# The input projection of a hybrid encoder layer by Strassen's seven products, on one core

## Chip, core and metric

One core of one Trainium2 chip runs the whole program. The metric is the device time of one execution in microseconds (us). The engines are named as the profile names them: PE (TensorE), DVE (VectorE), ACT (ScalarE), POOL (GpSimd), and SP (SyncE, which here only issues DMAs).

## What is computed

The reference is one encoder layer for 1024 tokens of width 2048, all in float32. Cut to what matters here:

```python
h = rmsnorm(x, norm_mix_g)                              # x: 1024 x 2048
proj = jnp.einsum('bsd,dn->bsn', h, w_in)               # w_in: 2048 x 6160
na_q, na_k, na_v, ml_q, ml_k, ml_v, ml_o, gates = jnp.split(proj, IN_SPLITS, axis=-1)
na_out = rmsnorm(neighbourhood_attention(na_q, na_k, na_v, rpb), na_norm_g)
ml_out = mlstm_mixer(ml_q, ml_k, ml_v, ml_o, gates, b_gates, conv_w, conv_b, ml_norm_g)
x = x + concatenate([na_out, ml_out]) @ w_out
x = x + expert_choice_ffn(rmsnorm(x, norm_ffn_g), w_router, w_gate, w_up, w_down)
return rmsnorm(x, final_norm_g)
```

The widths of the eight parts are 1024, 1024, 1024, 512, 512, 1024, 1024 and 16. The first seven make 6144 columns, 12 blocks of 512. Only this first projection, what it writes and the start of the attention behind it are changed.

## The kernel before

**Precision.** A float32 product is made of three products of a faster type (fp32r): each operand is split into a high part, a copy rounded to fp32r on ACT, and a low part, the difference of the value and the high part, on DVE. The product is high x high + high x low + low x high.

**The projection.** The activations a_hi and a_lo (16 pieces of 128 inputs by 1024 tokens) are made once at the start from xT, with the gain g_mix, and stay in SBUF. The scale 1/rms of each token (rstd) is applied when a result leaves PSUM. The weights stream through a ring of four tiles of 1024 columns (two pieces of 128 inputs x 512 columns): SP loads raw, ACT makes whi (`high`, L902), DVE makes wlo (`low`, L1226). There are 12 blocks of 512 columns in two kinds. Six are made in rows (`rows_block`, L1718 to L1720): activations are the stationary operand, weights move, the result has tokens on partitions, and ACT evicts it (L910). Six are made in features (`feats_block`, L1740): weights are stationary, activations move, the result has features on partitions, and DVE evicts it (L1329, L1333). Each block is 16 pieces x 8 PSUM banks x 3 = 384 matmuls with 512 moving columns. Between the two kinds stand the 96 gate matmuls (L1761). POOL's queue stores the evicted tiles to the DRAM tensors scr_rows and scr_feats (L656).

**Beside it.** In the first feature blocks DVE computes the gates' scans (L1258 to L1314) and in the last four the convolution of ml_q and ml_k: for each of 8 blocks of 128 features, one tensor_scalar (L1355) and four scalar_tensor_tensor (L1358) of 1024 elements, and a Silu on ACT.

**Behind it.** The neighbourhood attention reads q, k, v and the bias back from DRAM. SP waits for the last projection result before it issues the first of these loads:

```python
sp.wait_ge(S["bank_ready"], 8 * BLK)
for m in stsem:
    sp.wait_ge(m, 32 * (BLK - 2))
fetch_skew(0)
fetch_qk(0)
fetch_v(0)
```

The order of the work on each engine is the order in which the program text of that engine's function is written; semaphores join them. Nothing is reordered by a planner.

Of the kernel before, what the change touches and what calls it, by code (L numbers as in the profile page):

```python
# [16 lines left out]
P = 128  # L17
# [13 lines left out]
BW = 512  # L31
BLK = 12
ROWBLK = 6
# [20 lines left out]
MLU = 16 * MLH  # L54
ROOM = 19456
# [33 lines left out]
def trunk(nc, t):  # L89
    ctx = ExitStack()  # L90
    with ctx:
# [20 lines left out]
        proj = ExitStack()  # L112
        raw = sb("raw", [P, RING, 1024], F32, proj)
        whi = sb("whi", [P, RING, 1024], F32R, proj)
        wlo = sb("wlo", [P, RING, 1024], F32R, proj)
        stage = sb("stage", [P, 4, BW], F32, proj)
        t0 = sb("t0", [P, 1024], F32, proj)
        t1 = sb("t1", [P, 1024], F32, proj)
        t2 = sb("t2", [P, 1152], F32, proj)
        rstd_bc = sb("rstd_bc", [P, 1024], F32, proj)  # L120
        t3 = stage[:, 0:2, :].rearrange("p a b -> p (a b)")
        wide = ExitStack()
        a_hi = sb("a_hi", [P, KD, SEQ], F32R, wide)
        a_lo = sb("a_lo", [P, KD, SEQ], F32R, wide)
        gmix = sb("gmix", [P, KD], F32, wide)
        ssum = sb("ssum", [P, KD], F32, wide)
        wg_raw = sb("wg_raw", [P, GWC], F32, wide)
        wg_hi = sb("wg_hi", [P, GWC], F32R, wide)
        wg_lo = sb("wg_lo", [P, GWC], F32R, wide)
        wide.close()  # L130

        gate = ExitStack()
        gate.enter_context(nc.sbuf_tensor("under_wide", [P, 2 * KD * SEQ + 2 * KD + 3 * GWC], F32))
        g_bias = sb("g_bias", [P, 2], F32, gate)
        b_last = sb("b_last", [64, TT], F32, gate)
        c_last = sb("c_last", [64, TT], F32, gate)
        m_next = sb("m_next", [64, TT + 2], F32, gate)
        m_prev = sb("m_prev", [64, TT], F32, gate)
        m_end = sb("m_end", [64, TT], F32, gate)
        decay = sb("decay", [64, TT], F32, gate)  # L140
        cw = sb("cw", [P, 2, CONVW + 1], F32, gate)
        gate.close()


        proj.close()
# [96 lines left out]
        for n in ("const_in ident_done raw0 raw1 raw2 raw3 xt0 xt1 xnat0 xnat1 xn_sq hT_hi hT_lo w_hi w_lo w_used "  # L242
                  "bank_ready bank_staged st0 st1 st2 st3 stage_free meansq_done rstd_done rstd_out rstd_bc_in "
                  "wg_hi wg_done gates_ready gates_copied gpad_zero gb_in grows_out dve_step "
                  "act_step pool_step mask_done acc_free conv_in conv_free silu_done conv_out "
                  "pool_past dve_past pad_in rep_out cols_ready cols_out nq0 nq1 nkv0 nkv1 nb0 nb1 colm_in nmask_done "
# [13 lines left out]
        xhalf = [t2[:, 0:1024], rstd_bc[:, :]]  # L260
# [120 lines left out]
        def chunk_free(eng, b, m):  # L381

            if m >= 4:
                eng.wait_ge(S["w_used"], 7 * b + (m - 3))
            elif m < 3:
                eng.wait_ge(S["w_used"], 7 * b + (m - 2))
            else:
                eng.wait_ge(S["bank_ready"], 8 * b)
# [6 lines left out]
        def o_consumed(eng, q):  # L395

            i, k = q // KD, q % KD
            if k == KD - 1:
                eng.wait_ge(S["bank_ready"], 8 * BLK + 4 * i + 4)
            else:  # L400
                eng.wait_ge(S["w_used"], 7 * BLK + (KD - 1) * i + k + 1)
# [5 lines left out]
        def _(sp):  # L407
            def fetch(b, m):

                if not (isinstance(b, int) and b == 0 and m < 4):  # L410
                    sp.wait_ge(S["w_lo"], CPB * b + (m - 3))
                src = t["w_stream"][bass.ds(CPB * b + m, 1), :, :].rearrange("a p c -> (a p) c")
                sp.dma_start(raw[:, m % RING, :], src).then_inc(rawsem[m % RING], 16)

            sp.dma_start(gmix[:, :], t["g_mix"]).then_inc(S["const_in"], 16)
            sp.dma_start(wg_raw[:, 0:KD * 16], t["w_gates"]).then_inc(S["const_in"], 16)

            for m in range(CPB):
                fetch(0, m)
                for k in (2 * m, 2 * m + 1):  # L420
                    if k >= 2:
                        sp.wait_ge(S["hT_lo"], k - 1)
                    sp.dma_start((t0, t1)[k % 2][:, :], t["xT"][k * P:(k + 1) * P, :]).then_inc(xtsem[k % 2], 16)
            with sp.Fori(1, BLK) as b:
                for m in range(CPB):
# [1686 lines left out]
```

## Time and profile before

| what | value |
|---|---|
| median of 3 runs | 2973.68 us (2972.35 to 2974.95) |
| profiled execution: time | 2972.88 us |
| profiled execution: span | 2971.3 us |
| granted PE clock, mean | 0.973 |
| PE busy | 2781.7 us (94%) |
| DVE busy | 1583.1 us (53%) |
| ACT busy | 1324.5 us (45%) |
| POOL busy | 374.5 us (13%) |
| DMA, mean | 222 GB/s |

The profiled execution lasts 1.6 us longer than its span, which begins with the first instruction and ends with the last. A busy share is an average over stages with different limits, so the reader should look at the share of each engine in the stretch that is changed, here the first 1083 us.

### The profile page before, as it was taken

What the parts mean: (1) busy time and instruction counts of PE and PEld (TensorE: products, weight loads), DVE (VectorE), ACT (ScalarE), POOL (GpSimd) and SP (SyncE); (2) the same over time, 40 slices, a digit from 0 to 9 for tenths busy, and PEclk for the clock granted to TensorE, in tenths of its full rate; (3) what the DMA queues carried; (4) which work ended last, traced back from release to release, by engine and by line L of the source; (5) the groups of instructions that cost most, each with busy time, mean ns of one, the idle gap of its engine ahead of it and who ended that gap; (6) DMA issues with size and microseconds to landing.
All of it is one profiled execution on the core that took longest, in us unless ns stands there. A gap on an engine that the chain in (4) does not pass through costs nothing.

```text
span 2971.3 us, 33520 instructions
## 1 busy us (share of the span) xinstructions
PE 2781.7 (94%) x12738; PEld 2281.5 (77%) x12738; DVE 1583.1 (53%) x1679; ACT 1324.5 (45%) x1458; POOL 374.5 (13%) x593
## 2 busy tenths in 40 slices
PE   8999999999999989989999944999999999999992
PEld 7888888888888867768777733888888888888881
DVE  4110111311233326674332358888888888888883
ACT  5111111201111115654232323777777777777773
POOL 1200000020011023571010101010000000000000
PEclk9999999999999999999999977999999999999996
DMA  8322212122222238534354455999999999999987
GB/s 308 93 76 78 76 51 78 57 98 78 78 104 101 78 117 245 179 103 139 131 167 135 162 177 197 381 396 405 401 388 406 401 405 404 403 403 403 402 319 269
DMA packets 193516, 660.53 MB, mean 222 GB/s; under 512 B 24025, under 2 KB 49128, under 8 KB 170608
## 3 DMA queue, kind: packets, MB, share of 16 engines
q1 hardware_dynamic: 169088, 564.52, 50.2%
q0 software_dynamic: 24304, 94.39, 9.7%
q8 instruction: 74, 1.21, 0.2%
q14 instruction: 50, 0.41, 0.0%
HBM read 585.99 MB, written 72.79 MB: 222 GB/s over the span
## 4 chain that ended last, share of the span: by engine, by line
PE 87%; issue 4%; DVE 3%; POOL 3%; DMA 1%; SPq 1%; ACT 0%; POOLq 0%; DVEq 0%; ACTq 0%
PE ps L2024 23%; PE ps L1740 17%; PE ps L1718 6%; PE ps L1720 6%; PE ps L1719 6%; PE ps L1961 4%; PE ps L1963 4%; PE ps L1962 4%; PE ps L2047 4%; PE ps L2045 4%; PE ps L2046 4%; PE ps L2003 1%; PE ps L1942 1%; PE ps L1782 1%; PE ps L1761 1%
## 5 line engine op out<-in xcount | busy, mean ns | idle before, releaser
L1635 DVE TENSOR_TENSOR elo<-eraw,ehi 128x2048 fp32r<-128x2048 f32 x384 | 874.4, 2292 | 137.1 <-ACT ehi L1146 130.6
L1146 ACT ACTIVATE ehi<-eraw 128x2048 fp32r<-128x2048 f32 x384 | 733.2, 1919 | 246.8 <-PE ps L2024 163.8
L1226 DVE TENSOR_TENSOR wlo<-raw,whi 128x1024 fp32r<-128x1024 f32 x96 | 117.6, 1225 | 704.9 <-ACT whi L902 704.8
L902 ACT ACTIVATE whi<-raw 128x1024 fp32r<-128x1024 f32 x96 | 101.7, 1059 | 732.6 <-PE ps L1740 393.5
L2024 PE MATMUL ps<-ehi,xh 128*128 128x512 f32 x960 | 373.5, 389 | 0.0
L2024 PE MATMUL ps<-elo,xh 128*128 128x512 f32 x960 | 373.4, 389 | 0.0
L1718 PE MATMUL ps<-whi,a_hi 128*128 128x512 f32 x768 | 299.9, 390 | 11.3 <-DVE a_lo L1236 11.3
L1719 PE MATMUL ps<-wlo,a_hi 128*128 128x512 f32 x768 | 299.6, 390 | 0.0
L1720 PE MATMUL ps<-whi,a_lo 128*128 128x512 f32 x768 | 299.5, 390 | 0.0
L2024 PE MATMUL ps<-ehi,xl 128*128 128x512 f32 x960 | 256.6, 389 | 0.0
L1740 PE MATMUL ps<-a_hi,whi 128*128 128x512 f32 x768 | 236.8, 389 | 1.8 <-DVE t L1258 1.6
L1740 PE MATMUL ps<-a_lo,whi 128*128 128x512 f32 x768 | 236.5, 389 | 0.0
L1740 PE MATMUL ps<-a_hi,wlo 128*128 128x512 f32 x768 | 236.4, 389 | 0.0
L1509 DVE TENSOR_TENSOR olo<-oraw,ohi 128x512 fp32r<-128x512 f32 x128 | 88.5, 697 | 249.9 <-ACT ohi L1073 249.8
L2024 PEld LDWEIGHTS ps<-ehi,xl 128*128 128x128 f32 x960 | 180.2, 188 | 37.4
L2024 PEld LDWEIGHTS ps<-elo,xh 128*128 128x128 f32 x960 | 180.2, 188 | 37.4
L2024 PEld LDWEIGHTS ps<-ehi,xh 128*128 128x128 f32 x960 | 180.2, 188 | 37.4
L1961 PE MATMUL ps<-ohi,a_hi 128*128 128x512 f32 x512 | 204.9, 400 | 3.6 <-DVE mh L1469 3.6
L2045 PE MATMUL ps<-ehi,hh 128*128 128x512 f32 x512 | 202.9, 396 | 0.0
L1963 PE MATMUL ps<-ohi,a_lo 128*128 128x512 f32 x512 | 200.7, 392 | 0.0
L1962 PE MATMUL ps<-olo,a_hi 128*128 128x512 f32 x512 | 200.5, 392 | 0.0
L2047 PE MATMUL ps<-ehi,hl 128*128 128x512 f32 x512 | 199.5, 390 | 0.0
(246 smaller groups left out, 3892.3 us busy)
## 6 DMA issues: line engine op xcount, KB each, us to landing
eraw<-in_w_gate SPq DMA_DIRECT2D x256, 512.0 KB
eraw<-in_w_up SPq DMA_DIRECT2D x256, 512.0 KB
eraw<-in_w_down SPq DMA_DIRECT2D x128, 1024.0 KB
raw<-in_w_stream SPq DMA_DIRECT2D x96, 512.0 KB
oraw<-in_w_stream SPq DMA_DIRECT2D x128, 256.0 KB
scr_rows<-stage POOLq DMA_DIRECT2D x48, 256.0 KB, 2.3
scr_feats<-stage POOLq DMA_DIRECT2D x48, 256.0 KB, 2.3
t<-in_xT SPq DMA_DIRECT2D x16, 512.0 KB, 5.6
```

Of the source, the lines that this page charges most:

```text
L1146: act.activation(ehi[:, p % ERING, :], flat2(eraw[:, 2 * (p % EDEEP):2 * (p % EDEEP) + 2, :]), ACT.Copy)\
L1635: dve.tensor_tensor(elo[:, p % ERING, :], flat2(eraw[:, 2 * (p % EDEEP):2 * (p % EDEEP) + 2, :]), ehi[:, p % ERING, :].bitcast(F32), ALU.s ...
L1718: pe.matmul(ps[:, n, :], xs, hi, start=(k == 0), stop=False)
L1719: pe.matmul(ps[:, n, :], xs, lo, start=False, stop=False)
L1720: last = pe.matmul(ps[:, n, :], src_lo[:, k, n * P:(n + 1) * P], hi, start=False, stop=(k == KD - 1))
L1740: last = pe.matmul(ps[:, n, :], w, src[:, k, h * BW:(h + 1) * BW], start=(k == 0 and w is hi and src is a_hi), stop=(k == KD - 1 and w is lo))
L1961: pe.matmul(bank, xs, hi, start=(k == 0), stop=False)
L1962: pe.matmul(bank, xs, lo, start=False, stop=False)
L1963: last = pe.matmul(bank, a_lo[:, KORD[k], n * P:(n + 1) * P], hi, start=False, stop=(k == KD - 1))
L2024: last = pe.matmul(gu_bank(e, c), a[:, k, :], w[:, p % ERING, c * BW:(c + 1) * BW], start=(k == 0 and a is hi and w is ehi), stop=(k == KD ...
L2045: pe.matmul(y_bank(e, c), hh[:, h, :], ehi[:, p % ERING, at], start=(k == 0), stop=False)
L2047: last = pe.matmul(y_bank(e, c), hl[:, h, :], ehi[:, p % ERING, at], start=False, stop=(k == KE - 1))
```

## The change

**Strassen.** The projection is cut into 12 runs (`RUNS`). A run is one half of the tokens (512) and one pair of column blocks (1024 columns). With the input dimension cut into halves as well, it is a product of two 2 x 2 block matrices, made by seven products of half size instead of eight. A product i has 8 chunks k (128 inputs x 512 columns) and two token tiles: 8 x 2 x 3 = 48 matmuls. `B11` and `B22` are quarters of the weights that stay for a run; products 1, 2, 5 and 6 stream a chunk through a ring of four slots (wst) and add b11 or b22 to it; product 3 adds b22 to b11 in place; products 0 and 4 use b11 and b22 as they are (SUMMED is 1, 2, 3, 5, 6; g is the run, i the product, k the chunk):

```diff
+def sum_on_dve(g, i, k):
+    return i in SUMMED and k % 4 == 3 and g not in (0, 5, 6)
...
+        def weight_sum(eng, g, i, k):
...
+            a = weights_of(g, i, k)
+            other = b11[:, k, :] if i in (1, 2) else b22[:, k, :]
+            return eng.tensor_tensor(a, a, other, ALU.subtract if i in (2, 6) else ALU.add)
```

POOL makes 390 of these 480 sums, DVE 90. The sum is split into whi (ACT) and wlo (DVE) as before, now in tiles of 512 columns and a ring of four such tiles:

```diff
-    act.activation(whi[:, m % RING, :], raw[:, m % RING, :], ACT.Copy).then_inc(S["w_hi"], 1)
+    if q >= RING:
+        consumed(act, q - RING)
+    act.activation(whi[:, q % RING, :], weights_of(g, i, k), ACT.Copy).then_inc(S["w_hi"], 1)
...
-    dve.tensor_tensor(wlo[:, m % RING, :], raw[:, m % RING, :], whi[:, m % RING, :].bitcast(F32), ALU.subtract)
+    dve.tensor_tensor(wlo[:, q % RING, :], weights_of(g, i, k), whi[:, q % RING, :].bitcast(F32), ALU.subtract)
```

The activations' seven combinations for a token half are made in runs 0 (first half), 5 and 6 (second half): POOL multiplies xT by the gain (`gain`, 16 operations for a half), DVE and POOL add (`act_sum`, 8 and 12), ACT and DVE split (28 each). They lie in seven regions of SBUF (acts).

**Results.** A product ends in one of four pairs of PSUM banks. ACT copies three of the seven to SBUF (`keep_product`), DVE adds the others to them (`combine`, 16 operations of 128x512 in a run, one operand in PSUM), ACT multiplies by rstd (`stage_c`, 8 in a run). All runs are in rows. In the six feature runs PE turns each result by 32 transposes against the identity, ACT evicts them, and SP stores them:

```diff
+            def turn_c(g, c):
+                if is_rows(g):
+                    return
+                for t_ in range(2):
...
+                    for f in range(4):
...
+                        last = pe.transpose(bank, stage[:, 2 * (c % 2) + t_, f * P:(f + 1) * P], ident[:, :])
```

The matmuls of a chunk, and the gates, which are now 16 plain float32 matmuls for each half instead of 96 of fp32r:

```diff
-            with pe.Fori(1, ROWBLK) as b:
-                rows_block(b, a_hi, a_lo)
-            with pe.Fori(ROWBLK, BLK) as b:
-                feats_block(b)
+                for t_ in range(2):
+                    pe.matmul(bank, xh_, hi, start=(k == 0), stop=False)
+                    pe.matmul(bank, xh_, lo, start=False, stop=False)
+                    last = pe.matmul(bank, xl_, hi, start=False, stop=(k == 7))
...
+            for k in range(KD):
+                last = pe.matmul(gate_bank(6 * half_), wg[:, at:at + P], flat3(actr[region(half_, 6 - k // 8)][:, k % 8, :, :]),
+                                 start=(k == 0), stop=(k == KD - 1))
```

**Beside it.** The gates' scans stand in run 7, between its chunks 16 and 38. The convolution stands in runs 8 to 11, two feature blocks in each: one of its five operations behind each of the chunks 6 to 10, and 34 to 38:

```diff
+                if g >= CONVRUN:
+                    c, n = divmod(8 * i + k, 28)
+                    if 6 <= n < 11:
+                        conv(2 * (g - CONVRUN) + c, n - 6)
```

**Behind it.** The first loads of the attention wait for product 4 of the last run, no longer for the last product; the last three stores of results are issued behind them:

```diff
-            sp.wait_ge(S["bank_ready"], 8 * BLK)
+            sp.wait_ge(S["bank_ready"], 2 * (7 * (NRUN - 1) + 5))
             fetch_skew(0)
...
             fetch_v(1)
+            store_c(NRUN - 1, 1)
+            store_c(NRUN - 1, 2)
+            store_c(NRUN - 1, 3)
```

**The order on the engines.** DVE in a feature block with convolution before (wlo is a weight's low part, t is the convolution's accumulator):

```order
L1226 TENSOR_TENSOR wlo<-raw,whi 128x1024 x2
L1355 TENSOR_SCALAR t<-t,cw 128x1024
L1358 SCALAR_TENSOR_TENSOR t<-t,cw 128x1024 x4
L1226 TENSOR_TENSOR wlo<-raw,whi 128x1024 x2
L1355 TENSOR_SCALAR t<-t,cw 128x1024
L1358 SCALAR_TENSOR_TENSOR t<-t,cw 128x1024 x4
L1226 TENSOR_TENSOR wlo<-raw,whi 128x1024
L1333 TENSOR_TENSOR stage<-ps,rstd_bc 128x512 x8
```

And DVE now, from the start of one of the runs 8 to 11 (wst and b are a streamed and a kept chunk of weights, tmp_b and stage hold partial results):

```order
L1610 TENSOR_TENSOR wlo<-b,whi 128x512 x3
L1656 TENSOR_TENSOR tmp_b<-ps,tmp_b 128x512
L1658 TENSOR_TENSOR stage<-ps,stage 128x512
L1656 TENSOR_TENSOR tmp_b<-ps,tmp_b 128x512
L1658 TENSOR_TENSOR stage<-ps,stage 128x512
L1610 TENSOR_TENSOR wlo<-b,whi 128x512 x4
L1771 TENSOR_SCALAR t<-t,cw 128x1024
L1610 TENSOR_TENSOR wlo<-b,whi 128x512
L1774 SCALAR_TENSOR_TENSOR t<-t,cw 128x1024
L1610 TENSOR_TENSOR wlo<-wst,whi 128x512
L1774 SCALAR_TENSOR_TENSOR t<-t,cw 128x1024
L455 TENSOR_TENSOR wst<-wst,b 128x512
```

The five operations of a convolution no longer stand in one piece between tiles that serve 48 matmuls each; they stand between chunks that serve 6 matmuls each, and the additions of results and the weight sums have joined them.

POOL had only DMA issues in the projection; now, in run 0, it has gains (L894), weight sums (L455) and activation sums (L493):

```order
L894 TENSOR_SCALAR actr<-actr,gmix 128x512 x16
L455 TENSOR_TENSOR wst<-wst,b 128x512 x13
L493 TENSOR_TENSOR actr<-actr 128x2x256
L455 TENSOR_TENSOR wst<-wst,b 128x512
L493 TENSOR_TENSOR actr<-actr 128x2x256
L455 TENSOR_TENSOR wst<-wst,b 128x512
```

Every one of these stands ahead of a chunk or of an activation that PE waits for.

## Rows read from the trace of the kernel before

**Rows 1.** The page, part 1 (busy us, share of the span, instructions):

```profile
PE 2781.7 (94%) x12738; PEld 2281.5 (77%) x12738; DVE 1583.1 (53%) x1679; ACT 1324.5 (45%) x1458; POOL 374.5 (13%) x593
```

**Rows 2.** Windows: length; busy us of PE, PEld, DVE, ACT, POOL; clock; DMA:

```profile
240.00:530.00 290.00, 290.00 (x1281) 240.01 (x1280) 33.10 (x27) 48.37 (x54) 12.96 (x24) 1.00 0.20 70
...
530.00:600.00 70.00, 68.41 (x300) 55.96 (x299) 27.59 (x32) 19.95 (x22) 8.88 (x17) 1.00 0.19 71
```

**Rows 3.** PE's timeline and the chain of waits: start, duration, what:

```profile
2.42 6.23 DMA t<-in_xT
...
11.29 0.77 PE L1718 MATMUL ps<-whi,a_hi 128*128 128x512 f32 x1 [11.29 <-DVE a_lo L1236]
...
536.01 22.24 PE ps L1761 x96
...
1739.60 3.62 PE ps L1942 x8
...
1821.42 3.66 PE ps L2003 x16
...
2824.43 43.52 PE ps L2024 x192
```

**Rows 4.** The end of the projection and the start of the attention, timeline:

```profile
1082.23 0.61 PE L1740 MATMUL ps<-a_hi,wlo 128*128 128x512 f32 x2
1095.85 4.18 PE L1782 MATMUL ps<-nak,naq 128*128 128x384 f32 x6 [13.00 <-DMA nak<-scr_feats]
...
1090.25 0.99 POOL L757 TENSOR_TENSOR bias<-skew,nmask 128x384 f32<-128x384 f32 x1
...
1098.42 0.61 ACT L1004 ACTIVATE prob<-prob,ntop 128x384 f32<-128x384 f32 x1 [55.59 <-DVE ntop L1386]
```

**Rows 5.** Groups by line, DVE (busy us, mean ns, idle before and its releaser):

```profile
L1226 DVE TENSOR_TENSOR wlo<-raw,whi 128x1024 fp32r<-128x1024 f32 x96 | 117.6, 1225 | 704.9 <-ACT whi L902 704.8
L1509 DVE TENSOR_TENSOR olo<-oraw,ohi 128x512 fp32r<-128x512 f32 x128 | 88.5, 697 | 249.9 <-ACT ohi L1073 249.8
L1333 DVE TENSOR_TENSOR stage<-ps,rstd_bc 128x512 f32<-128x512 f32 x32 | 21.4, 689 | 59.6 <-PE ps L1740 50.9 <-POOLq L660 8.2
L1358 DVE SCALAR_TENSOR_TENSOR t<-t,cw 128x1024 f32<-128x1024 f32 x32 | 41.1, 1285 | 1.1
```

**Rows 6.** Groups by line, POOL and ACT:

```profile
L757 POOL TENSOR_TENSOR bias<-skew,nmask 128x384 f32<-128x384 f32 x48 | 46.6, 1002 | 59.9 <-DMA skew<-scr_rpb_rep 59.4
L812 POOL TENSOR_TENSOR qs<-qs,mq 128x1024 f32<-128x1024 f32 x2 | 4.7, 2365 | 0.0
L798 POOL TENSOR_SCALAR mh<-mh,rsm 128x256 f32<-128x256 f32 x16 | 8.8, 553 | 0.1
L806 POOL TENSOR_SCALAR na_out<-na_out,nrs 128x1024 f32<-128x1024 f32 x8 | 9.3, 1174 | 0.0
L1073 ACT ACTIVATE ohi<-oraw 128x512 fp32r<-128x512 f32 x128 | 80.7, 631 | 258.6 <-PE ps L1963 258.5
```

**Rows 7.** Timeline, DVE beside POOL, in the mLSTM stage:

```profile
1252.29 0.73 POOL L801 TENSOR_TENSOR mh<-mh,mo 128x256 f32<-128x256 f32 x1
...
1252.65 0.64 DVE L1482 SCALAR_TENSOR_TENSOR mh<-mh,rsm,mo 128x256 f32<-128x256 f32 x1
1252.99 0.55 POOL L769 TENSOR_SCALAR kw<-kn,cols 128x128 f32<-128x128 f32 x1
...
1320.02 1.12 POOL L806 TENSOR_SCALAR na_out<-na_out,nrs 128x1024 f32<-128x1024 f32 x1
1320.07 1.21 DVE L1434 TENSOR_TENSOR qkw<-st,wexp 128x128 f32<-128x128 f32 x1 [0.19 <-POOL wexp L778]
```

**Rows 8.** The instructions of L1434, L769 and L1482: ns min/median/max, and when they start:

```profile
L1434 DVE TENSOR_TENSOR qkw<-st,wexp x64: 282/293/1205, 1218.1 to 1329.5; 128x128 f32<-128x128 f32 x64
...
L769 POOL TENSOR_SCALAR kw<-kn,cols x56: 363/372/547, 1205.2 to 1325.7; 128x128 f32<-128x128 f32 x56
...
L1482 DVE SCALAR_TENSOR_TENSOR mh<-mh,rsm,mo x16: 485/634/968, 1252.7 to 1339.6; 128x256 f32<-128x256 f32 x16
```

More of the change, by code:

```diff
@@ L111, in trunk @@
         sb("even", [P, 64])
[L112 to L145, printed above, removed]
         def place(at, *items):
@@ new lines, in sum_done, with slot, streamed, weights_of @@
+        def sum_done(eng, g, i, k):
+            if sum_on_dve(g, i, k):
+                eng.wait_ge(S["w_sum_v"], SUMS_V[chunk(g, i, k)])
+            else:
+                eng.wait_ge(S["w_sum_p"], SUMS_P[chunk(g, i, k)])
+        def slot(g, i, k):
+            return wst[:, k % RING, :]
+        def streamed(eng, g, i, k):
+            eng.wait_ge(rawsem[k % RING], 16 * ((32 * g + STREAMED[i] + k) // RING + 1))
+        def weights_of(g, i, k):
+            if i in (0, 3):
+                return b11[:, k, :]
+            return b22[:, k, :] if i == 4 else slot(g, i, k)
@@ L407, in _, with w_block, fetch_b11 @@
         def _(sp):
[L408 to L413, printed above, removed]
+            def w_block(b, m):
+                return t["w_stream"][CPB * b + m, :, :]
+            def fetch_b11(g, m):
+                if g:
+                    sp.wait_ge(S["w_lo"], chunk(g - 1, 3, 2 * m + 1) + 1)
+                    sp.wait_ge(wbsem[m], 32 * g)
+                sp.dma_start(flat3(b11[:, 2 * m:2 * m + 2, :]), w_block(2 * RUNS[g][1], m)).then_inc(wbsem[m], 16)
@@ new lines, in gain, with row_scale @@
+            def gain(half_, k):
+                pool.wait_ge(rxsem[k // 2], 64 * half_ + 64)
+                for b in range(2):
+                    a = flat3(actr[region(half_, 6 - b)][:, k, :, :])
+                    pool.tensor_scalar(a, a, gmix[:, 8 * b + k:8 * b + k + 1], 0.0, ALU.mult, ALU.add).then_inc(S["x_gained"], 1)
+            def row_scale(half_):
+                four = slice(4 * half_, 4 * half_ + 4)
+                pool.wait_ge(S["meansq_done"], half_ + 1)
+                pool.tensor_tensor(rstd[:, four], meansq[:, four], half[:, 0:4], ALU.pow).then_inc(S["rstd_done"], 1)
+                pool.wait_ge(S["rstd_done"], half_ + 1)
+                pool.dma_start(t["rstd_d"][half_ * BW:(half_ + 1) * BW].rearrange("(t p) -> p t", p=P), rstd[:, four],
+                               allow_slow_non_contiguous=True).then_inc(S["rstd_bc_in"], 16)
@@ L923, in _ @@
-            for m in range(3):
-                high(1, m)
-            act.wait_ge(S["rstd_done"], 1)
-            evict_rows(0)
-            for first, end, func in ((1, ROWBLK - 2, ACT.Copy), (ROWBLK - 2, ROWBLK, ACT.Sigmoid)):
-                with act.Fori(first, end) as b:
-                    for m in range(3, CPB):
-                        high(b, m)
-                    for m in range(3):
-                        high(b + 1, m)
-                    evict_rows(b, func)
-            high(ROWBLK, 3)
@@ L955, in _ @@
-            for m in range(3):
-                high(ROWBLK + 2, m)
-            def feats_high(b, last):
-                for m in range(3, CPB):
-                    high(b, m)
-                    if m in (5, 7):
-                        q = (m - 5) // 2
-                        act.wait_ge(S["conv_free"], 2 * b + (q - 2 * (ROWBLK + 2) + 2))
-                        act.activation(t0[:, :], t0[:, :], ACT.Silu, bias=cw[:, q, CONVW:CONVW + 1]).then_inc(S["silu_done"], 1)
-                if not last:
-                    for m in range(3):
-                        high(b + 1, m)
@@ L1275, in _, with gates_sum @@
+            def gates_sum(x):
+                r, way = ways[x]
                 dve.tensor_tensor_scan(out=t1[r, ::way], data0=t3[r, :], data1=t1[r, ::way], initial=0.0,
```

1090 lines of the change are left out of this document (727 added, 363 removed).

## The prediction

> **What bounds the kernel now.** I read the page first. PE is busy for 94% of the span, DVE for 53%, POOL for 13% [rows 1]. The average says little, so I went to the windows: from 240 to 530 us PE is busy for all of the 290 us at the full clock, DVE for 33 and POOL for 13 [rows 2]. The groups by line say the same from the other side: DVE sits idle 704.9 us before wlo, waiting for ACT [rows 5], and ACT in turn waits for PE to free the ring. So the projection is a row of matmuls that nothing delays. The timeline puts it from 11.3 to 1082.8 us [rows 3, 4], 1071.5 us. A matmul costs 43.52/192 = 0.2267 us [rows 3]; 4608 of them and the 22.24 us of gates make 1066.9, so 4.6 us are lost in stalls. Behind it PE stands still for 13 us, until nak has landed, and the first softmax runs at 1098.4 [rows 4].
>
> **PE's work.** Strassen takes 12 x 7 x 48 = 4032 matmuls in place of 4608: 576 x 0.2267 = 130.6 us less. The features are turned by 6 x 4 x 8 = 192 transposes of 128x128; 16 such take 3.66 us [rows 3], so they add 43.9. The gates were 22.24; now they are 32 plain float32 matmuls of 512 columns. Four of that kind (each leaves two records) take 3.54 to 3.62 us [rows 3], so 0.89 each and 28.3 in all, 6.1 more. PE's work falls by 130.6 - 43.9 - 6.1 = 80.6 us. If nothing held PE up, that would be the gain, and the 4.6 us of stalls besides.
>
> **What each run asks of DVE and POOL.** A run is 336 matmuls, 76.2 us, 83.5 with its 32 transposes. DVE makes 56 lows and, in the nine runs where it helps, 10 sums, 66 x 0.697 = 46.0 (olo is the same form [rows 5]), and 16 additions of results at 0.689 [rows 5], 11.0: 57.0 us. POOL makes 30 sums there, 40 in runs 0, 5 and 6. For a 128x512 sum I interpolate between 1.002 for 384 and 2.365 for 1024 elements [rows 6]: 1.275 us, 38 or 51 us a run. ACT makes 56 highs at 0.631 [rows 6], 35, and some 14 to 22 copies of like size, 10 to 15: below 52 us, not the bound. Taken one by one, every engine fits under PE.
>
> **They are not independent.** At 1320.07 a DVE operation with two SBUF inputs, whose median is 0.293 us [rows 8], takes 1.21: POOL began a 1.12 us one at 1320.02, and DVE ends 0.14 us after it [rows 7]. The other triple shows both ways: DVE, begun at 1252.65 during POOL's mh, ends 0.27 after POOL, and POOL's kw, begun at 1252.99, ends 0.25 after DVE, in 0.55 in place of 0.37 [rows 7, 8]. So the two exclude each other while they stream, and only the first 0.12 to 0.16 of each is hidden. By that a waiting low takes its streaming time after POOL's end, 0.53 us (512 elements more cost 1.225 - 0.697 [rows 5]), and a waiting sum 1.275 - 0.12 = 1.155 after DVE's: 1.69 us a pair. A chunk of PE's is 6 x 0.2267 = 1.36 us. Additions from PSUM have one SBUF input; such DVE operations are not held, and POOL can work beneath them.
>
> The page SBUF — State Buffer of the Trainium skill (section SBUF: two separate sides) has a rule that speaks against this change: GpSimd and a DVE operation with two SBUF inputs take one port pair in turn, as an exclusive lock "held for the full instruction". The trace agrees that they take turns, but not that the whole time counts: DVE ended 0.14 us after POOL where it takes 0.293 alone [rows 7, 8]. Taken in full, a pair would cost 1.97 us, not 1.69.
>
> **The stalls, run by run.** Each is the time by which DVE with its waits exceeds PE's 76.2 or 83.5. A wait for a sum can cost DVE nothing (it falls into idle time or an addition) up to 1.155. POOL holds the pair for about 45% of a run, so I take 0.65 to 0.8 a sum, 20 to 24 us.
> - Runs 1 and 2 (rows): 57.0 + 22 = 79 us, 3 over each; the ring is only four chunks, 4.1 us ahead. Together **6**.
> - Runs 3 and 4 (features): 79 lies under 83.5, but the summed products come in blocks of three and two: 1.5 each, **3**.
> - Runs 8 and 9: a convolution is 4 x 1.285 [rows 5] and a tensor_scalar near 0.7, two a run, 11.7: 91 against 83.5, **15** for both. Runs 10 and 11 are in rows: 89 against 76.2, **26**. Before, this work was free: DVE had the time of 48 matmuls for each tile.
> - Run 7: from 530 to 600 DVE is busy 27.6 us [rows 2], of which four lows and one gate copy are not the scans; 22 us are. They stand in chunks 16 to 38. 79 + 22 less 3 of lead: 98, **22**.
> - Run 5: DVE 56 lows, 8 activation sums and 12 splits, 76 x 0.69 + 11 = 63.6; POOL 40 sums and 16 gains. A gain of 512 elements lies between 0.553 for 256 and 1.174 for 1024 [rows 6]; 0.57 of it holds DVE. POOL: 46.2 + 9.1 = 55.3. The two add up to 119, less 11 beneath additions and 5 of hidden starts: 103, **20**.
> - Run 6: DVE 72 x 0.69 + 11 = 60.8, POOL 52 x 1.155 = 60: 121 less 17 is 104, against 83.5 + 14.2 of gates, **6**.
> - Run 0: xT of the first half and b11 are 6 MB, and 1.5 MB are needed before a pair of chunks; the first load took 6.23 us [rows 3]. I put the first matmul at 13, product 0's end at 41 where PE needs 11 (four loads, gains, two sets of splits), and the rest at 10 to 14 a product: end at 131. PE's work is 90.4 and its start was 11.3: **29**.
>
> Sum 127. Stage: -80.6 - 4.6 + 127 = +42 us.
>
> **The start of the attention.** The loads now run during the last two products (21.8 us), so the 13 us gap goes. Next late is the bias: POOL begins it only after its last sums and ACT's last four stagings, some 5 us after PE's end, and its first took until 8.4 us after it before [rows 4]. The first softmax ran 15.6 after; I put it at 8, a gain of 8 (nothing at least, 13 at most).
>
> The three stores that go behind the loads, and the results' DMAs that leave POOL's queue for SP's, cost nothing as long as the streams stay ahead; a slot of the ring is filled again only after its low, which is the third rival's case.
>
> **Forecast.** 2972.9 + 42 - 8 = **3007 us**, 1.1% slower. The sum is against the profiled execution; the median is 0.8 us above it, which I leave out.
>
> **The rivals.**
> 1. **The waits fall into slack (faster).** DVE's additions (11 us), its idle time (19.2 us of 76.2 in an assisted run) and the transposes swallow most of POOL's 34.7 us. Then runs 1 to 4 cost nothing, 5 and 6 half, 7 to 11 some 25 in place of 63 (DVE alone: 68.7 us in a run with convolution), run 0 about 20: 58. -85.2 + 58 - 8 = -35: **2938**. The point is a wait of 0.4 us a sum. For it: POOL runs ahead during products 0 and 4, which have no sums. Against: two of three chunks it works for are in blocks, at 1.69 a pair against 1.36.
> 2. **Little but the start stalls.** Run 0's 20 and 8 for the gates: -85.2 + 28 - 8 = -65, **2908**. It needs the pair to exclude nearly nothing, against [rows 7].
> 3. **The ring of streamed chunks is too short.** A slot's cycle is issue and load, about 3 us (half of the first load's 6.23 for half its size [rows 3]), sum with wait 1.7, high 0.63, low with wait 1.3: 6.6, or 1.66 a chunk against 1.36. With other loads in between it is 7.5, and the 24 chunks not loaded ahead in a run (products 1, 2, 5, 6) lose 0.5 each less the lead of 4.1 twice: 4 us a run, 48 more: **3055**. By the page's full lock 0.28 more for each of 390 pairs would give up to 109; half of it hidden, 3060, the same case.
>
> **Chances.** Forecast 0.48, ring or full lock 0.12, waits in slack 0.26, little stalls 0.05; 0.09 lies between, near no change. A measurement of this kernel can tell about 0.2% (6 us) from no change. Faster 0.33, same 0.08, slower 0.59. The range, 2932 to 3055, holds the first rival and reaches to the third; the forecast's own range is 2985 to 3035. A tenth lies below it (run 0's start and gates alone), a tenth above.
>
> **What would show it.** In the profile after: the projection ends near 1125 us; PE is idle in each run, released by wlo, mostly in runs 0, 5 and 7 to 11; lows run from 0.69 up to 1.8 us, with a mean above 1.0 in products 1 to 3; POOL is busy for over 550 us. It is wrong if the mean low stays below 0.8 us, or if PE waits for DMAs. If the stage ends before 1083 us with lows over 1.0 us, the lock is right and the slack was undersized. If the first softmax does not come within 10 us of PE's last projection matmul, the last term is wrong.

## The result, and the profile after

The changed kernel takes **3246.5 us** (median of 4 runs, 3235.1 to 3248.9) against 2973.0 for the kernel before (4 runs on the same chip): a ratio of **1.091, 95% interval 1.089 to 1.094**. The forecast was 3007, at most 3055. The direction was right, the size was not: +273 us where +34 were forecast. The profiled execution lasts 3235.1 us, its span 3233.4.

The page's part 1 of the changed kernel, to be held against [rows 1]:

```profile
PE 2791.2 (86%) x12322; PEld 2194.8 (68%) x12322; DVE 2328.2 (72%) x2547; ACT 1726.9 (53%) x2236; POOL 952.9 (29%) x930
```

POOL has 578 us more to do and DVE 745, and no engine is busy for the whole span. The windows say it more sharply: the first is that of [rows 2], the second is run 2 alone, the third run 0 (length; busy us of PE, PEld, DVE, ACT, POOL; clock; DMA):

```profile
240.00:530.00 290.00, 255.90 (x1074) 195.97 (x1073) 214.03 (x252) 136.90 (x227) 149.66 (x123) 0.99 0.49 156
...
269.30:364.70 95.40, 81.82 (x338) 61.48 (x337) 71.04 (x83) 44.34 (x71) 51.59 (x48) 1.00 0.48 156
14.00:161.30 147.30, 105.70 (x368) 73.07 (x369) 104.79 (x107) 62.66 (x110) 86.49 (x81) 0.90 0.43 145
```

In run 2 DVE is busy for 71 of 95 us, ACT for 44, POOL for 52, and PE is late all the same: it needs 76.2. So no engine is the bound of the whole run; it waits for a chain that goes through several of them. The groups by line show the links of that chain (busy us, mean ns | idle before and releaser):

```profile
L455 POOL TENSOR_TENSOR wst<-wst,b 128x512 f32<-128x512 f32 x312 | 455.8, 1474 | 605.2 <-DMA wst<-in_w_stream 604.0
L455 POOL TENSOR_TENSOR b<-b 128x512 f32<-128x512 f32 x78 | 119.8, 1559 | 0.2
L455 DVE TENSOR_TENSOR wst<-wst,b 128x512 f32<-128x512 f32 x72 | 66.9, 929 | 84.0 <-DMA wst<-in_w_stream 79.0 <-DMA b<-in_w_stream 4.7
L1202 ACT ACTIVATE whi<-wst 128x512 fp32r<-128x512 f32 x384 | 236.4, 629 | 352.5 <-POOL wst L455 252.4 <-PE ps L2188 76.4 <-DVE wst L455 22.5
L1610 DVE TENSOR_TENSOR wlo<-wst,whi 128x512 fp32r<-128x512 f32 x384 | 382.9, 1023 | 138.5 <-ACT whi L1202 131.3
L1610 DVE TENSOR_TENSOR wlo<-b,whi 128x512 fp32r<-128x512 f32 x288 | 268.3, 953 | 104.1 <-ACT whi L1202 102.8
L2186 PE MATMUL ps<-whi,acts 128*128 128x512 f32 x1344 | 572.6, 426 | 256.2 <-DVE wlo L1610 236.4
```

The last link stands among the waits of SP's queue from 14 to 1338 us (us in total, times, longest); L596 is the load of a streamed chunk:

```profile
SPq L596 <- DVE wlo L1610: 726.2, 335, 22.6
```

Read it from the top: POOL waits for the slot's load, ACT for POOL's sum, DVE for ACT's high, PE for the low; and the load waits for the low that frees the slot. Before, DVE had sat 704.9 us idle in front of its lows [rows 5]; now a ready low is itself late, 1.02 us on average in place of 0.69.

Over a run DVE is not full, but in product 3, whose eight sums stand in a row with its lows, it is. DVE's window in run 2 (length, busy us; clock; DMA):

```profile
306.00:321.00 15.00, 15.00 (x12) 1.00 0.38 126
```

From the first low of product 3 to the first of product 4 DVE is busy for all of 14.3, 12.7 and 12.7 us in runs 2, 3 and 4; in product 1 for less than half of 15 to 17 us.

The price of a pair came out as forecast. Timelines of DVE and of POOL in run 3 (start, length, what, count):

```profile
399.90 1.16 DVE L455 TENSOR_TENSOR wst<-wst,b 128x512 f32<-128x512 f32 x1 [1.78 <-DMA wst<-in_w_stream]
400.99 5.13 DVE L1610 TENSOR_TENSOR wlo<-wst,whi 128x512 fp32r<-128x512 f32 x3
406.04 1.76 DVE L1610 TENSOR_TENSOR wlo<-b,whi 128x512 fp32r<-128x512 f32 x1
```

```profile
400.48 10.17 POOL L455 TENSOR_TENSOR b<-b 128x512 f32<-128x512 f32 x6
```

Three lows in 5.13 us and six sums in 10.17: 1.70 us a pair (forecast 1.69; 1.97 by the full lock that the prediction took from the page SBUF — State Buffer of the Trainium skill, whose section Terms has the words it quotes; the trace does not bear out the 1.97). This is the alternation of [rows 7], now wherever POOL's sums and DVE's lows stand in a row.

The transposes cost less than half of the forecast. The 3.66 us for 16 of them [rows 3] belong to a stretch at the 1.2 GHz level. A window of the kernel before over them, and the next 16 in its timeline:

```profile
1821.40:1825.10 3.70, 3.65 (x16) 3.27 (x16) 1.60 (x3) 1.79 (x3) 0.00 (x0) 0.52 1.03 420
1851.13 1.91 PE L2003 MATMUL ps<-ident,xg 128*128 128x128 f32 x16
```

And eight in the changed kernel, with the matmul behind them:

```profile
458.16 1.03 PE L2228 MATMUL ps<-ident,stage 128*128 128x128 f32 x8
458.95 0.48 PE L2186 MATMUL ps<-whi,acts 128*128 128x512 f32 x1
```

That is 0.79 us from start to start, 0.1 us each: all 192 take some 20 us, not 43.9. With 27 us for the gates (28.3 forecast) and 4032 x 0.2267 = 914 for the products, PE's own work in the stage is 962 us, not the forecast's 986 (1066.9 less 80.6).

The stage ran from 14.1 to 1338.1, 1324 us, so 362 us are stalls, where 127 were forecast. (The first expectation below says 338, by the forecast's price of a transpose.) The attention then starts like this (timelines of PE, ACT and SP's queue), which answers to [rows 4]:

```profile
1337.85 0.39 PE L2188 MATMUL ps<-whi,acts 128*128 128x512 f32 x1
1339.34 2.17 PE L2272 MATMUL ps<-nak,naq 128*128 128x384 f32 x6 [1.10 <-DMA nak<-scr_feats]
1362.40 0.87 PE L2280 MATMUL ps<-ident,prob 128*128 128x128 f32 x3 [20.89 <-ACT prob L1387]
```

```profile
1357.07 1.50 ACT L1250 ACTIVATE stage<-tmp_b,rstd 128x512 f32<-128x512 f32 x2 [16.23 <-DMA scr_rows<-stage]
...
1361.55 0.61 ACT L1387 ACTIVATE prob<-prob,ntop 128x384 f32<-128x384 f32 x1 [1.67 <-DVE ntop L1855]
```

```profile
1347.15 7.55 SPq L724 DMA_DIRECT2D nav<-scr_rows  x16
1354.74 4.18 SPq L617 DMA_DIRECT2D scr_rows<-stage  x6
```

The idle 13 us before the first qk are gone, as forecast. But ACT stands for 16.2 us, because the store that frees its stage (L617) is issued behind three families of loads on SP's queue. The first softmax comes 23.4 us after PE's last projection matmul; before it was 15.6.

By run, from my own tally of PE's first matmuls in the timeline (us; the forecast is PE's need plus the stall of the prediction; run 0 counts from the first matmul, forecast at 13):

```
run          0      1      2      3     4     5     6     7     8     9     10    11
forecast     118    79     79     85    85    104   104   98    91    91    89    89
after        147.3  107.9  95.4   95.7  96.4  120.9 108.7 122.6 108.0 105.6 104.6 110.6
```

Every run is longer than forecast, by 5 us (run 6) to 29 us (runs 0 and 1), although the feature runs 3 to 6, 8 and 9 were given 4 to 6 us too much for their transposes.

### The profile page after: what moved, and what is told of

Same layout as the page of the kernel before. It is cut to its first block, busy times and chain, and to the rows that moved or that the text cites. A ratio compares the mean times of both kernels' runs of the same rounds, so it can differ in the third digit from the quotient of the medians.

```text
span 3233.4 us, 35665 instructions
## 1 busy us (share of the span) xinstructions
PE 2791.2 (86%) x12322; PEld 2194.8 (68%) x12322; DVE 2328.2 (72%) x2547; ACT 1726.9 (53%) x2236; POOL 952.9 (29%) x930
## 4 chain that ended last, share of the span: by engine, by line
PE 50%; issue 21%; POOL 16%; DVE 6%; DMA 3%; SPq 2%; ACT 1%; POOLq 0%; ACTq 0%; DVEq 0%
PE ps L2515 22%; POOL wst L455 9%; PE ps L2452 4%; PE ps L2454 4%; PE ps L2453 4%; PE ps L2538 3%; PE ps L2537 3%; PE ps L2536 3%; POOL b L455 2%; DVE wlo L1610 2%; DMA wst<-in_w_stream 1%; PE ps L2494 1%; PE ps L2433 1%; POOL actr L493 1%; PE ps L2292 1%
## 5 line engine op out<-in xcount | busy, mean ns | idle before, releaser
L2186 PE MATMUL ps<-whi,acts 128*128 128x512 f32 x1344 | 572.6, 426 | 256.2 <-DVE wlo L1610 236.4
L455 POOL TENSOR_TENSOR wst<-wst,b 128x512 f32<-128x512 f32 x312 | 455.8, 1474 | 605.2 <-DMA wst<-in_w_stream 604.0
L2186 PEld LDWEIGHTS ps<-whi,acts 128*128 128x128 f32 x1344 | 261.9, 195 | 414.5 <-DVE wlo L1610 281.7
L2187 PE MATMUL ps<-wlo,acts 128*128 128x512 f32 x1344 | 542.5, 404 | 0.0
L2188 PE MATMUL ps<-whi,acts 128*128 128x512 f32 x1344 | 541.1, 403 | 0.0
L1610 DVE TENSOR_TENSOR wlo<-wst,whi 128x512 fp32r<-128x512 f32 x384 | 382.9, 1023 | 138.5 <-ACT whi L1202 131.3
L1202 ACT ACTIVATE whi<-wst 128x512 fp32r<-128x512 f32 x384 | 236.4, 629 | 352.5 <-POOL wst L455 252.4
L1610 DVE TENSOR_TENSOR wlo<-b,whi 128x512 fp32r<-128x512 f32 x288 | 268.3, 953 | 104.1 <-ACT whi L1202 102.8
L1202 ACT ACTIVATE whi<-b 128x512 fp32r<-128x512 f32 x288 | 176.8, 627 | 247.2 <-PE ps L2188 165.0
L2188 PEld LDWEIGHTS ps<-whi,acts 128*128 128x128 f32 x1344 | 262.7, 195 | 59.5
L2187 PEld LDWEIGHTS ps<-wlo,acts 128*128 128x128 f32 x1344 | 263.1, 196 | 46.1 <-issue 0.5
L1456 ACT ACTIVATE ohi<-oraw 128x512 fp32r<-128x512 f32 x128 | 80.7, 631 | 258.3 <-PE ps L2454 258.3
```

Of the source, the lines that this page charges most:

```text
L455: return eng.tensor_tensor(a, a, other, ALU.subtract if i in (2, 6) else ALU.add)
L1202: act.activation(whi[:, q % RING, :], weights_of(g, i, k), ACT.Copy).then_inc(S["w_hi"], 1)
L1610: dve.tensor_tensor(wlo[:, q % RING, :], weights_of(g, i, k), whi[:, q % RING, :].bitcast(F32), ALU.subtract)\
L2186: pe.matmul(bank, xh_, hi, start=(k == 0), stop=False)
L2187: pe.matmul(bank, xh_, lo, start=False, stop=False)
L2188: last = pe.matmul(bank, xl_, hi, start=False, stop=(k == 7))
```

## The experiments

Theory A: DVE's lows wait for POOL's sums at SBUF. Theory B: the four slots of streamed chunks are too few (rival 3). Beside these: the scale's readback on POOL's queue (6), the stores behind the loads (4), the convolution (9), and what lets a DVE operation in between POOL's (13, 14). The kernel before had medians of 2972.0 to 2972.6 us in these comparisons. Most experiments have two executions, and the four of the changed kernel lie 14 us apart; the profiled one is the fastest of them. So a difference of medians under some 10 us shows nothing, and where one is 18 to 25 us, the traces' own difference is given beside it.

**1. Sums of 8 columns** (only 8 of 512 columns of each weight sum are computed):

```diff
-return eng.tensor_tensor(a, a, other, ...)
+return eng.tensor_tensor(a[:, 0:8], a[:, 0:8], other[:, 0:8], ...)
```

> The 480 weight sums add only the first 8 of their 512 columns (the rest of the sum is left out); waits, loads and order stay. Theory A, POOL's sums hold the ports that DVE's lows need: the lows fall from a mean of 1.0 to 0.7 us, PE's stalls in the projection fall from 338 us to 60 to 100, and the time is about 2980 us (2960 to 3010). Theory B, the slot of a streamed chunk comes round too late because of its load (3.0 us) and the steps behind it: only 1.3 us of a cycle of 7 to 8 goes, the stalls fall by a fifth, about 3180 us.

Measured: **3041.0 us**, ratio 1.023 (1.021 to 1.025), 205 us less than the change, over half of the 362 us of stalls. The lows are back at 0.70 and 0.73 us as theory A has it, but the time is 31 us above its range: by the trace the stage still lasts 1125 us, 163 more than PE's work. This run alone does not say whether the gain came by the ports or by the sum's length in the chain; experiment 10 tells them apart in part.

**2. Five slots** in place of four for the streamed chunks (`SRING = 5`, with its semaphores).

> Five slots for streamed weight chunks in place of four, nothing else. Theory B (slot cycle too long): products 1, 2, 5 and 6 go from 14.9 us on average towards 12.5, some 100 us in all, about 3140 us. Theory A (ports): POOL and DVE have no more time than before, the gain is under 30 us, about 3225 us.

Measured: **3201.9 us**, 45 less, between the two theories. Rival 3's 48 us were the right size, but they are a part of the loss beside the first, not in its place.

**3. All sums on DVE**, made one chunk ahead:

```diff
-return i in SUMMED and k % 4 == 3 and g not in (0, 5, 6)
+return i in SUMMED
```

> All 480 weight sums on DVE, each one chunk ahead of its low; POOL keeps gains and activation sums. Theory A: a sum costs the pair 0.69 us on DVE in place of 1.15 on POOL and nobody waits for the other; DVE alone needs 96 x 0.69 + 11 = 77 us a run, so the time falls by 100 to 170 us, to 3080 to 3150. Theory B: with four slots the cycle stays (load 3.0, sum 0.7, high 0.6, low 0.7), and DVE itself now waits for loads, so no gain or a loss, 3230 us or more.

Measured: **3098.7 us**, 148 less, although DVE has 390 x 0.695 = 271 us more to do itself. The groups:

```profile
L455 DVE TENSOR_TENSOR wst<-wst,b 128x512 f32<-128x512 f32 x384 | 266.7, 695 | 93.0 <-DMA wst<-in_w_stream 90.3
L1610 DVE TENSOR_TENSOR wlo<-wst,whi 128x512 fp32r<-128x512 f32 x384 | 266.6, 694 | 44.8 <-ACT whi L1202 42.8
```

An engine that does both loses less than two that keep each other out: 1.39 us for a low and a sum, against 1.70.

**4. The three stores in front of the second head pair's loads** on SP's queue:

```diff
+            store_c(NRUN - 1, 1)
+            store_c(NRUN - 1, 2)
+            store_c(NRUN - 1, 3)
             fetch_skew(1)
             fetch_qk(1)
             fetch_v(1)
-            store_c(NRUN - 1, 1)
-            store_c(NRUN - 1, 2)
-            store_c(NRUN - 1, 3)
```

> The last three stores of results are issued after the first head's loads and ahead of the second head's. Theory: ACT's last staging, and behind it POOL's bias and the first softmax, waited for a store that stood behind 26 more DMA issues on SP; the first softmax comes 10 to 12 us earlier and the time falls by about 11 us to 3235 us. Rival: the second head's loads are late by as much and the gain is given back at head 1, no change.

Measured: **3228.2 us**, 18 less. By the trace it is 12: the first softmax comes 11.6 us after PE's last projection matmul in place of 23.4. PE's wait for it falls from 20.9 to 6.1 us.

**5. All sums on POOL** (`sum_on_dve` returns False).

> All 480 weight sums on POOL (90 more there, none on DVE). Theory A (ports): each moved sum costs the pair 1.15 us in place of 0.69, in the nine runs that had help: about 90 x 0.46 = 41 us and some more waiting, 3280 to 3300 us. Rival: POOL has 605 us of idle time and DVE is the busier engine, so DVE's relief of 62 us wins, 3190 to 3230 us.

Measured: **3252.5 us**, 6 more, by neither expectation and no difference that the runs show. The lows grow from 1023 and 953 to 1172 and 1143 ns, 114 us in all, but DVE is rid of 90 sums that took 97, and the two nearly cancel. Where the kernel puts these 90 makes next to no difference.

**6. The scale's readback issued by SP**, not by POOL:

```diff
-                if g < 2 and (i, k) == (3, 3):
-                    row_scale_back(g)
+                if g < 2:
+                    ...
+                    sp.dma_start(t2[:, 0:BW], t["rstd_d"][...].partition_broadcast(P))
```

> The readback of 1/rms (runs 0 and 1, product 3) is issued by SP and no longer waited for by POOL in front of five or six weight sums. In run 0 POOL waited 7.0 us there and in run 1 10.2, and DVE's low waited 18 us in run 0 behind POOL's burst that followed. Theory: product 3 of runs 0 and 1 falls from 40.1 and 25.7 to below 28 and 17 us, 15 to 25 us in all, about 3225 us. Rival: the chunk ring hides it or SP's own wait delays the streams of product 5, under 5 us.

Measured: **3222.0 us**, 25 less; by the trace the stage is 17 us shorter. Run 1 falls from 107.9 to 97.7, its product 3 from 25.7 to 14.4; run 0 from 147.3 to 141.6. In the changed kernel all of POOL's sums stood behind this wait:

```profile
93.97 0.59 POOL L910 DMA_DIRECT2D t<-scr_rstd_d  x1 [7.01 <-DMA scr_rstd_d<-rstd]
```

In run 1 the same wait takes 10.2 us.

**7. Both 1 and 2.**

> The sums add only 8 of 512 columns (the rest is left out) and there are five slots. Both causes lightened at once. If the ports and the slot cycle are one chain (a slot is held by load, sum, high and low alike), the two gains do not add up: 3041 less 10 to 20 us, about 3025. If they are separate, the 45 us of the five slots come in full: 2996.

Measured: **2988.9 us**, 52 less than experiment 1, where experiment 2 had given 45 without it: the two causes add, as the second expectation (2996) had it. And here a run without any loss can be seen, run 2 in a window (columns as above):

```profile
232.00:308.00 76.00, 76.00 (x337) 62.86 (x336) 47.39 (x83) 43.89 (x71) 19.48 (x49) 1.00 0.60 194
```

336 matmuls in 76.2 us by the tally: the forecast's price for a product's matmuls holds to a tenth of a microsecond. Run 3, with 16 transposes, took 77.9 us here, below the 83.5 that the forecast gave a feature run.

**8. Everything repaired:** all sums on DVE, five slots, stores in front, scale through SP.

> All weight sums on DVE, five slots, the last stores ahead of the second head's loads, the readback of 1/rms on SP; the whole computation. From the runs so far 3099 less 18 for the stores, 30 to 50 for the slots (DVE waited 88 us for loads) and 10 for the readback: about 3025 us (3005 to 3045). It is faster than 2972 only if DVE's waits were nearly all of what is left, which its 77 us a run beside PE's 76 to 83 speaks against.

Measured: **3037.6 us**, ratio 1.022 (1.021 to 1.024): 209 us better than the change, and still slower than the kernel before. The stage lasts 1138 us by the trace, 176 more than PE's work.

**9. Convolution on 8 of 1024 columns** (the rest of its multiply and multiply-adds is left out):

```diff
-dve.tensor_scalar(t0[:, :], t2[:, 0:1024], cw[:, c % 2, 0:1], None, ALU.mult)
+dve.tensor_scalar(t0[:, 0:8], t2[:, 0:8], cw[:, c % 2, 0:1], None, ALU.mult)
```

> Leaves out most of the convolution: its multiply and three multiply-adds work on 8 of their 1024 columns. My theory, that in runs 8 to 11 DVE is behind PE and the 11.7 us of a convolution are paid for in full: runs 8 to 11 fall from 108.0, 105.6, 104.6 and 110.6 us to about 95 each, runs 0 to 7 stay within 1 us, total 3195 to 3210 us. Rival, that these operations lie in time in which DVE waits for sums anyway: runs 8 to 11 lose under 4 us each, total above 3230 us.

Measured: **3223.5 us**, 23 less; by the trace the stage is 12 us shorter. Runs 8 to 11: 104.5, 102.5, 102.5, 102.4, together 17 us less, 4 a run, nearer the rival than my theory. Run 3, which has no convolution, took 102.0 in place of 95.7, so a few us in one run show little. The convolution mostly lies in time in which DVE waits anyway.

**10. Sums that only write.** Each of POOL's sums is a memset of its 512 columns; the sum is left out.

```diff
+if not sum_on_dve(g, i, k):
+    return eng.memset(a, 0.01)
```

> Leaves the sums of POOL out: each is one memset of the same 512 columns, which writes SBUF and reads nothing; I estimate 0.5 us from 0.95 for 1024 columns in the profile of the changed kernel. If POOL keeps DVE out only while it reads SBUF, the lows come down to about 0.70 us, as with the sums of 8 columns (0.70 and 0.73), and the total is 3040 to 3065 us, the rest of the sum's length being 0.2 us more in the chain. If a write keeps DVE out as well, the mean low rises to 0.8 to 0.95 us and the total to 3070 to 3120 us.

Measured: **3058.0 us**, ratio 1.029 (1.027 to 1.031).

```profile
L456 POOL MEMSET wst<- 128x512 f32 x312 | 163.9, 529 | 790.9 <-DMA wst<-in_w_stream 787.9
...
L1612 DVE TENSOR_TENSOR wlo<-wst,whi 128x512 fp32r<-128x512 f32 x384 | 258.5, 704 | 137.2 <-ACT whi L1204 136.0
L1612 DVE TENSOR_TENSOR wlo<-b,whi 128x512 fp32r<-128x512 f32 x288 | 199.7, 708 | 123.0 <-ACT whi L1204 120.9
```

POOL works on SBUF for 0.53 us at every chunk, and the lows are back at 0.70: a write of POOL's does not hold DVE, so what holds it is that the sums read. The page SBUF — State Buffer (section Who interferes with whom) of the Trainium skill says the same of a DVE instruction with two SBUF inputs: GpSimd contends with it through an instruction that reads SBUF, not through one that only writes it. The memset is 0.2 us longer than the sum of 8 columns and costs 17 us. By that rate a sum of 1.26 us that kept nobody out would add some 60 us more, and the other 130 of the 188 between this kernel and the change would be the ports. Both are estimates: no run has a sum of full length beside which DVE is free.

**11. The repaired version, with every fourth sum of runs 7 to 11 on POOL.**

> The repaired version (all sums on DVE, five slots, stores in front, scale through SP) with every fourth sum of runs 7 to 11 back on POOL. Each such sum frees DVE of 0.70 us and, where it overlaps with a low or a sum of DVE, gives 0.5 us back: 50 sums, so 10 us less at best, 3027 us. Rival, that one operation of POOL makes both engines wait as in the changed kernel: 0.3 us a sum lost, 3050 us. I expect 3030 to 3042.

Measured: **3053.6 us** (ratio 1.028, 1.026 to 1.029), 16 more than experiment 8, as the rival had it or worse: fifty sums on POOL cost 0.3 us each.

**12. The floor:** sums of 8 columns, five slots, stores in front, scale through SP.

> Leaves the sums out but for 8 of 512 columns, with five slots, stores in front and the scale through SP: what this split of work reaches if a sum costs next to nothing. From the five-slot version with tiny sums (2988.9 us), the stores' 18 us and the scale's 25 us if they add: 2946 us, 0.9% under the kernel before. If they do not add, since run 0 had lost its starved low with the tiny sums already: 2965 to 2975 us, no faster than before. I expect 2950 to 2972.

Measured: **2964.5 us**, ratio 0.998 (0.997 to 0.999). With the sums all but left out this arrangement is 0.24% faster than the kernel before. By the trace its stage lasts 1063 us, so 101 us of stalls are left without the sums' length: 27 in run 0, 21 in run 7, beside the gates' scans, 16 in run 5. Experiment 8, with 480 real sums of 0.69 us on DVE, lies 73 us above. So no version was found that beats the kernel before with all of its work done.

**13 and 14. What lets DVE in.** The changed kernel has five DVE operations of 6 to 18 us in the projection, all where POOL's row of operations begins behind an issue of a DMA on its queue. Experiment 13 puts a small such issue ahead of product 3's sums in six runs, experiment 14 a memset of 4 columns in the same place:

```diff
+if g in (2, 3, 4, 8, 9, 10) and (i, k) == (3, 0):
+    pool.dma_start(even[:, 4 * g:4 * g + 4], t["conv_wb"][0, :, 0:4]).then_inc(S["spare"], 16)
```

> One small load (4 columns of a constant into a tile nobody reads) is issued on POOL's queue ahead of the first sum of product 3 in runs 2, 3, 4, 8, 9 and 10. Theory F, that DVE is passed over when POOL's row of sums begins behind an issue of a DMA: in each of the six runs one DVE operation of over 4 us (6 to 10) stands there, POOL's sums beside it take 1.25 us each in place of 1.70, and these runs grow by 2 to 6 us each, 15 to 35 us in all. Rival G, that something else decides (how the operations happen to meet): no new operation over 4 us in runs 2 to 4, the median within 10 us of 3246.5.

> The control of the run with the extra issue: at the same six places a memset of 4 columns on POOL, about 0.15 us, in place of the load. Theory F: no DVE operation over 4 us beside the five known ones, the median within 10 us of 3246.5. Rival G, that any gap in POOL's row of sums can do it: DVE operations over 4 us in some of runs 2 to 4 here too.

Measured: **3263.8 us** with the issue (ratio 1.098, 1.094 to 1.103), **3242.1 us** with the memset (1.091, 1.088 to 1.094). Run 2, POOL and DVE with the issue:

```profile
308.82 0.56 POOL L1001 DMA_DIRECT2D even<-in_conv_wb  x1
309.39 7.37 POOL L455 TENSOR_TENSOR b<-b 128x512 f32<-128x512 f32 x6
```

```profile
309.34 9.17 DVE L1612 TENSOR_TENSOR wlo<-wst,whi 128x512 fp32r<-128x512 f32 x3
318.44 1.75 DVE L1612 TENSOR_TENSOR wlo<-b,whi 128x512 fp32r<-128x512 f32 x1
```

and with the memset:

```profile
308.37 0.11 POOL L1001 MEMSET even<- 128x4 f32 x1
308.42 10.14 POOL L455 TENSOR_TENSOR b<-b 128x512 f32<-128x512 f32 x6
```

```profile
308.90 5.13 DVE L1612 TENSOR_TENSOR wlo<-wst,whi 128x512 fp32r<-128x512 f32 x3
```

With the issue POOL's six sums take 7.37 us, 1.23 each, as if alone, and the first of DVE's three lows stands for 7.97 us, until they are through. With the memset the two alternate. At all six places with the issue a DVE operation stands like this, for 5.4 to 9.2 us; with the memset at none of them. (In runs 8 to 10 the convolution's own issues follow four sums later, and there DVE stands before and after.) Runs 2 to 4 take 102 us against 96 to 99, and the whole 22 us more (two executions each, 16 us apart at the least). Theory F holds at these places.

## Why the prediction was right or wrong

- **PE's work, -80.6 us: it fell by 24 us more.** The price of the products is right: a run is 76.2 us when nothing disturbs it (experiment 7), and product 4, which has nothing to sum, takes 10.9 us in runs 0 to 4 of the changed kernel too. But the 43.9 us of transposes came from a row at the 1.2 GHz level; at the full clock they took 20. In all PE's work fell by 105. Without this slip the forecast would have been 2983, further from what was measured.
- **The price of a pair, 1.69 us: right** (1.70). The full lock's 1.97, and with it that part of the third rival, did not show. The wait per POOL sum, taken as 0.65 to 0.8, was if anything too high: the 672 lows last 651.2 us in place of 672 x 0.69 = 464, and DVE's sums and splits of activations wait some 50 more; by 390 sums that is 0.6 us each.
- **The step that failed** is "Each is the time by which DVE with its waits exceeds PE's 76.2 or 83.5". In run 2 DVE was to need 79 us and was busy for 71, and the run took 95.4. A run's sum of busy time was not the limit. What counts is, product by product, the chain of one chunk, load, sum, high, low and the slot's next load; the four streamed products of run 2 take 12.3 to 15.5 us, a slot's round of 6.2 to 7.8 us where PE needs 5.4. Only in product 3 DVE itself is full, and the time that it has left in the others does not help there. Each link had grown by its wait, the engines work in order, and a late chunk is not made up. I wrote this cycle down in rival 3 (6.6 to 7.5 us) and set it against the forecast as an alternative, where it adds: five slots give 45 us with the sums and 52 without. The sums' own part, 205 us (experiment 1), alone exceeds the 127 that I had for all stalls; by the estimates of experiment 10 some two thirds of it are the ports and a third the sum's length in the chain.
- **The lead of four chunks** absorbed less than I took. I had let "3 over each" be the loss of runs 1 and 2; it was 32 and 19.
- **Runs 8 to 11** were right in mechanism only in part: DVE's sum of 89 to 91 us (91 for all four, by the prediction's own terms) was not what they took (105 to 111), and taking the convolution out gives 4 us, not 11.7.
- **Run 0** took 147.3 us from its first matmul, 118 forecast. What the forecast left out are the readback on POOL's queue and one low of 18.1 us (below). Run 5 (17 over) has no readback; its product 3, with splits and gains, took 30.9 us.
- **The clock** was not in the forecast. Before, the projection's window shows 1.00. After, the granted clock is 0.90 in run 0 and, by a window, 0.95 from 14 to 1338 us: behind some stalls of PE it is at the 1.2 GHz level for a while, so a stall can cost more than its own length. By my tally 203 matmuls of the stage stand 0.43 us apart in place of 0.23, which makes 41 of the 362 us.
- **The start of the attention, -8 us: wrong sign, +8.** The gap before qk did go. "The three stores that go behind the loads ... cost nothing" failed: 12 us by the trace, 18 by the medians (experiment 4).

In sum: the stage ended at 1338 in place of 1125, 213 us later (some 235 of stalls too few and 24 of transposes too many), and the attention's start was 16 us worse than thought; that accounts for the 228 us between 3007 and the profiled execution. Of the signs given in advance, a mean low over 1.0 us in products 1 to 3 (1.14), POOL over 550 us and PE released by wlo came true; the end near 1125 and lows of at most 1.8 us did not. PE itself never waited for a DMA in the projection's products; POOL did in its place, 604 us. What stays open is how the 362 us divide among the causes where they overlap. Single changes give 148 to 205, 45, 25, 23 and 18 by the medians; the repairs of experiment 8 together leave 176 us of stalls, and 101 even with the sums all but left out, of which experiment 12 shows only in which runs they lie.

## What to carry to other kernels

When work is added beside an engine that was never late, do not stop at each engine's busy time: follow one item through load, every engine and back to its free slot, and compare that cycle, divided by the number of slots, with the consumer's pace. Two engines that shut each other out were worse here than one that does both jobs (1.70 us a pair against 1.39), and a DMA issue at the head of the one's row made it worse still. A price read from a row of the trace needs the granted clock of that row beside it. And a trade of PE time for elementwise sums must first pay for the sums: here 12.5% fewer matmuls were worth 0.24% with sums that cost next to nothing. On a queue that runs in order, a store that frees a buffer goes in front of loads that nobody needs yet.

## What the runs showed of the hardware that I had not expected

**A waiting DVE operation can be passed over many times.** DVE's and POOL's timelines in run 0:

```profile
96.55 18.14 DVE L1610 TENSOR_TENSOR wlo<-b,whi 128x512 fp32r<-128x512 f32 x1 [7.23 <-ACT whi L1202]
```

```profile
95.80 1.27 POOL L493 TENSOR_TENSOR actr<-actr 128x512 f32<-128x512 f32 x1
97.02 1.26 POOL L455 TENSOR_TENSOR b<-b 128x512 f32<-128x512 f32 x1
...
103.12 6.14 POOL L493 TENSOR_TENSOR actr<-actr 128x512 f32<-128x512 f32 x5
109.23 4.91 POOL L455 TENSOR_TENSOR wst<-wst,b 128x512 f32<-128x512 f32 x4
```

The low, begun at 96.55, ends only with POOL's row of operations, 18.1 us later, while POOL goes at 1.22 us an operation as if alone. Four further DVE operations of 6.1 to 7.3 us stand behind POOL's DMA issues of the convolution. Experiments 13 and 14 show that an issue put at the head of POOL's row does it where nothing stood before; with a memset there the two alternate. It lasts until POOL has nothing to do for a moment. Not every row behind an issue does it: in run 2 these three sums follow seven issues of L953, take 1.56 us each, and no DVE operation beside them is over 2.0 us:

```profile
316.86 4.68 POOL L455 TENSOR_TENSOR wst<-wst,b 128x512 f32<-128x512 f32 x3
```

Why an issue does this, and not each time, no run here shows. Experiment 6 took the readback from POOL but left the store's issue, and its low took 20.6 us. With all weight sums on DVE no low is over 1.8 us, but the activation sums that POOL keeps do the same to other operations, in experiment 3 to this one, and in experiment 8, the repaired version, to a weight sum of 9.59 us:

```profile
96.28 9.81 POOL L493 TENSOR_TENSOR actr<-actr 128x512 f32<-128x512 f32 x8
98.31 8.33 DVE L1619 TENSOR_TENSOR acts<-actr,acts 128x512 fp32r<-128x512 f32 x1 [9.73 <-ACT acts L1220]
```

**The clock can fall after a short stall.** PE's timeline in run 3:

```profile
402.79 0.50 PE L2186 MATMUL ps<-whi,acts 128*128 128x512 f32 x1 [2.14 <-DVE wlo L1610]
...
403.59 0.49 PE L2186 MATMUL ps<-whi,acts 128*128 128x512 f32 x1
403.87 0.63 PE L2187 MATMUL ps<-wlo,acts 128*128 128x512 f32 x1
404.30 0.63 PE L2188 MATMUL ps<-whi,acts 128*128 128x512 f32 x1
```

After 2.1 us idle, matmuls that follow each other at 0.23 us stand 0.43 apart for 3 us; the window says 0.50 of the clock, the 1.2 GHz level:

```profile
403.80:406.80 3.00, 3.00 (x8) 2.22 (x7) 3.00 (x3) 0.63 (x1) 3.00 (x3) 0.50 0.26 83
```

It does not follow each such stall: run 2 lost 19 us in stalls, one of them of 2.4 us, and its window shows 1.00.

**A write of 2 KB in pieces of 4 bytes** (scr_rstd_d, 512 values) landed 10.2 and 11.8 us after its issue in runs 0 and 1, and POOL stood for 7.0 and 10.2 of them. A 256 KB load of the stream takes 3.0 us (median).
